# Forty modulation sums handed out anew over three stages of a two-block network

## What is computed

```python
def modulate(x, cond, norm_g, w_ada, b_ada):
    shift, scale, gate = jnp.split(jax.nn.silu(cond) @ w_ada + b_ada, 3, axis=-1)
    return rms_norm_2(x, norm_g) * (1 + scale) + shift, gate

h, gate = modulate(x, c, ...)        # condition c
hc, gate_c = modulate(xc, c_ctx, ...)  # condition c_ctx; its gate is not used
```

```python
def sq_relu_mlp(h, w_up, w_down):
    return jnp.square(jax.nn.relu(h @ w_up)) @ w_down
```

## The kernel before

| place | tiles | sums |
|---|---|---|
| rec_out, behind step j = 0, 1, 2, 3 | 0 to 3 | 1 each |
| up0, units 0 and 1 | 4, 5 | 1 each |
| up0, units 3, 5, ... 13 (loop) | 6 to 11 | 2 each |
| up0, units 14 and 15 | 12, 13 | 1 each |
| down0, m = 0 and 1, two tiles each | 14 to 17 | 2 each, so 4 per m |
| down0, m = 2 to 7 | 18 to 23 | 2 each |

## Time and profile before

### The profile page before, as it was taken

How to read it: one execution, slowest core, us unless ns; L and a number is a source line. 1 busy time by engine, 2 the same in 40 slices (tenths; PEclk the granted TensorE clock), 3 DMA queues, 4 the chain that set the end, 5 groups by cost and what they waited for, 6 DMA issues and landing times.

```text
span 894.3 us, 17915 instructions
## 1 busy us (share of the span) xinstructions
PE 864.8 (97%) x6992; PEld 822.3 (92%) x6992; DVE 686.5 (77%) x1072; ACT 473.1 (53%) x697; POOL 132.9 (15%) x154
## 2 busy tenths in 40 slices
PE   6999999999999997899999999999999999999998
PEld 5998999999999985599999999989899899999998
DVE  4896678889977688667676667677758998997793
ACT  7783355555443356755655444363367556636641
POOL 6220000012311000000000122232203222013000
PEclk9999999999999997999999999999999999999999
DMA  9754576679998432045655656556545554645542
GB/s 346 249 193 157 185 253 225 232 261 289 283 262 208 155 131 95 1 142 185 209 194 188 212 191 189 186 182 210 167 143 165 166 175 133 187 145 188 182 149 95
DMA packets 46960, 167.86 MB, mean 188 GB/s; under 512 B 5776, under 2 KB 5920, under 8 KB 46640
## 3 DMA queue, kind: packets, MB, share of 16 engines
q1 hardware_dynamic: 40896, 146.82, 49.8%
q0 software_dynamic: 5856, 20.00, 7.9%
q10 hardware_dynamic: 144, 0.15, 0.1%
HBM read 165.50 MB, written 1.44 MB: 187 GB/s over the span
## 4 chain that ended last, share of the span: by engine, by line
PE 73%; DVE 14%; issue 5%; ACT 5%; DMA 2%; DVEq 0%; ACTq 0%; SPq 0%
PE bank L560 20%; PE bank L562 19%; PE bank L561 19%; PE bank L627 5%; DVE wlo L1327 4%; ACT whi L967 2%; DVE ada_prod L1487 2%; DVE ada_prod L1511 2%; PE bank L645 2%; PE bank L787 1%; DVE tq L1543 1%; PE bank L882 1%; PE bank L892 1%; DMA raw<-weights 1%; PE bank L841 1%
## 5 line engine op out<-in xcount | busy, mean ns | idle before, releaser
L1327 DVE TENSOR_TENSOR wlo<-raw,whi 128x1024 fp32r<-128x1024 f32 x260 | 319.9, 1264 | 95.9 <-ACT whi L967 94.8
L560 PE MATMUL bank<-xh,whi 128*128 128x256 f32 x1328 | 374.9, 282 | 4.6 <-DVE vv L1923 1.5
L562 PE MATMUL bank<-xh,wlo 128*128 128x256 f32 x1328 | 369.7, 278 | 0.0
L561 PE MATMUL bank<-xl,whi 128*128 128x256 f32 x1328 | 369.7, 278 | 0.0
L967 ACT ACTIVATE whi<-raw 128x1024 fp32r<-128x1024 f32 x260 | 265.6, 1052 | 141.9 <-PE bank L562 104.2
L560 PEld LDWEIGHTS bank<-xh,whi 128*128 128x128 f32 x1328 | 249.2, 188 | 15.3 <-issue 8.6
L561 PEld LDWEIGHTS bank<-xl,whi 128*128 128x128 f32 x1328 | 249.3, 188 | 0.2
L562 PEld LDWEIGHTS bank<-xh,wlo 128*128 128x128 f32 x1328 | 249.3, 188 | 0.0
L560 PE MATMUL bank<-hhi,whi 128*128 128x256 f32 x512 | 142.4, 278 | 1.2 <-DVE wlo L1327 1.2
L562 PE MATMUL bank<-hhi,wlo 128*128 128x256 f32 x512 | 142.1, 278 | 0.0
L561 PE MATMUL bank<-hlo,whi 128*128 128x256 f32 x512 | 141.9, 277 | 0.0
(11 more groups left out here) (283 smaller groups left out, 1038.2 us busy)
## 6 DMA issues: line engine op xcount, KB each, us to landing
raw<-weights SPq DMA_DIRECT2D x260, 512.0 KB, 4.5
ada_raw<-ada_w POOLq DMA_DIRECT2D x24, 512.0 KB, 4.6
plain<-plain_w SPq DMA_DIRECT2D x16, 512.0 KB, 7.0
relB<-rel_scratch POOLq DMA_DIRECT2D x8, 256.0 KB, 7.3
bl<-rpb_in POOLq DMA_DIRECT2D x32, 64.0 KB, 3.7
x<-x_in SPq DMA_DIRECT2D x4, 256.0 KB, 6.2
cond<-cond_in POOLq DMA_DIRECT2D x1, 1024.0 KB, 7.8
cx<-ctx_in POOLq DMA_DIRECT2D x1, 1024.0 KB, 8.2
```

The source lines that it names most:

```text
L560: mmul(dst, hi, rh, start=start, stop=False)
L561: mmul(dst, hi, rlo, start=False, stop=False)
L562: return mmul(dst, lo, rh, start=False, stop=stop)
L1327: V_.tensor_tensor(wlo[:, sl], raw[:, sl], whi[:, sl].bitcast(F32), ALU.subtract)\
```

## The change

The total of 40 sums stays. The eight gate rows, which need one condition, all stand beside `rec_out`: tiles 0 and 1 ahead of step 0, then two behind each of the steps 0, 1 and 2, none behind step 3. `up0` gets one row of two conditions in each odd unit (tiles 8 to 15), and each tile of `down0` one row of two conditions (tiles 16 to 23). POOL loads tiles 2 to 9 in a row, then `cx`, then tiles 10 to 17.

```diff
-ADA_ORDER = [16, 17, 18, 19, 20, 21, 0, 1, 2, 3, 4, 5, 22, 23, 6, 7, 8, 9, 10, 11, 12, 13, 14, 15]
+ADA_ORDER = [16, 17, 18, 19, 20, 21, 22, 23, 0, 1, 2, 3, 4, 5, 6, 7, 8, 9, 10, 11, 12, 13, 14, 15]
-ADA_DOWN = [[14, 15], [16, 17], [18], [19], [20], [21], [22], [23]]
+ADA_UP, ADA_DOWN = 8, 16
...
-            for i in range(2, 6):
+            for i in range(2, ADA_UP + 2):
                 load_ada(i)
 
             pool.wait_ge(S_["chunk_used"], 2 * U0["up0"])
             pool.dma_start(cx[:], ctx_in).then_inc(S_["ctx_loaded"], 16)
-            quads(pool, U0["up0"], U0["up0"] + NUNITS["up0"], lambda q, r: load_ada_beside(q, r, U0["up0"]))
+            for i in range(ADA_UP + 2, ADA_DOWN + 2):
+                load_ada(i)
...
                 if isinstance(q, int):
-                    ada_tile({0: 4, 1: 5, 14: 12, 15: 13}[q * 4 + r - u0])
+                    if n % 2:
+                        ada_tile(ADA_UP + n // 2)
...
+            ada_tile(0)
+            ada_tile(1)
             for j in range(4):
                 add_to_x("rec_out", j, x[:, 2 * j:2 * j + 2])
                 x_lo(2 * j, "g_mlp0", 8 + 2 * j + 1)
                 x_lo(2 * j + 1, "g_mlp0", 8 + 2 * j + 2)
                 add_pair(0, j)
-                ada_tile(j)
+                if j < 3:
+                    ada_tile(2 * j + 2)
+                    ada_tile(2 * j + 3)
...
                     if name == "0":
-                        ada_tile(ADA_DOWN[m][0])
+                        ada_tile(ADA_DOWN + m)
...
-                    if name == "0" and len(ADA_DOWN[m]) > 1:
-                        ada_tile(ADA_DOWN[m][1])
```

More of the change, by code:

```diff
@@ L385, in load_ada @@
                 pool.dma_start(ada_raw[:, i % 2], ada_w[i]).then_inc(s_adaw[i % 2], 16)
[L387 to L396, removed]
             def zero_acc(k):
@@ L461, in load_rel_bias @@
                     .then_inc(S_["rel_bias_loaded"], 16)
[L463 to L466, removed]
             def add_ctx_squares(m):
@@ L479, in ahead_of_tile @@
                 add_ctx_squares(m)
-                if ADA_DOWN[m][0] + 2 < ADA_M:
-                    load_ada(ADA_DOWN[m][0] + 2)
+                if ADA_DOWN + m + 2 < ADA_M:
+                    load_ada(ADA_DOWN + m + 2)
             pool.dma_start(wiw[:], wi_in).then_inc(S_["wi_loaded"], 16)
             pool.wait_ge(S_["rel_stored"], 16)
-            squares_by_tile(3, 0, ahead_of_tile, behind_tile)
+            squares_by_tile(3, 0, ahead_of_tile, load_rel_bias)
             pool.dma_start(caus[:], c_caus).then_inc(S_["caus_loaded"], 16)
@@ L1501, in ada_beside @@
             def ada_beside(q, r, u0):
+                n = q * 4 + r - u0
                 if isinstance(q, int):
-                    ada_tile({0: 4, 1: 5, 14: 12, 15: 13}[q * 4 + r - u0])
+                    if n % 2:
+                        ada_tile(ADA_UP + n // 2)
                 elif r % 2:
-                    q0, a = u0 // 4 + 1, r // 2
-                    dve.wait_ge(s_adaw[a], q * 16 + 16 * (4 - q0))
-                    dve.wait_ge(S_["ada_used"], q * 2 + (6 + a - 2 * q0))
+                    q0, h = u0 // 4 + 1, r // 2
+                    i0 = ADA_UP + 1 + h
+                    dve.wait_ge(s_adaw[i0 % 2], q * 16 + 16 * (i0 // 2 + 1 - q0))
+                    dve.wait_ge(S_["ada_used"], q * 2 + (i0 - 2 * q0))
                     for c in range(2):
-                        V_.tensor_tensor_reduce(ada_prod[:], ada_raw[:, a], cond[:, c], 1.0, 0.0, ALU.mult, ALU.add,
+                        V_.tensor_tensor_reduce(ada_prod[:], ada_raw[:, i0 % 2], cond[:, c], 1.0, 0.0, ALU.mult, ALU.add,
                                                 ada_pair[:, c:c + 1]).then_inc(S_["ada_summed"], 1)
-                        dve.wait_ge(S_["ada_summed"], q * 4 + (2 * a + c + 1 - 4 * q0))
-                    V_.tensor_copy(ada[:, bass.ds(q * 2 + (a - 2 * q0), 1), :], ada_pair[:].unsqueeze(1))\
+                        dve.wait_ge(S_["ada_summed"], q * 4 + (2 * h + c + 1 - 4 * q0))
+                    V_.tensor_copy(ada[:, bass.ds(q * 2 + (1 + h - 2 * q0), 1), :], ada_pair[:].unsqueeze(1))\
                         .then_inc(S_["ada_used"], 1)
+            ada_tile(0)
+            ada_tile(1)
             for j in range(4):
```

## The result

The changed kernel took 896.81 us (median of 5, 896.31 to 898.25), the kernel of before 903.3 us (median of 5, 901.63 to 905.06): a ratio of 0.9932, 95% interval 0.9918 to 0.9945. (The ratios here are estimates of the record from all single times, not quotients of two medians.) Yet the two profiles don't differ by six microseconds anywhere.

What follows compares the result with a forecast made beforehand. VectorE was taken to set the time from 103 to 230 us, TensorE after. Gains of 1.0 us into up0 and 1.3 in down0, less 0.6 in up0's last unit, gave -1.7 us: 903.3 to 901.6 us, range 898.0 to 904.6.

Steps and rivals of the forecast that it cites:

- What bounds the kernel: From 103 to 230 us VectorE sets the time, though TensorE looks full; from 230.66 us TensorE does.
- rec_out, four sums at no cost: In rec_out, four more sums fit VectorE's waits for TensorE; the last ends before step 3 wants VectorE at 100.69 us.
- L: Time from issue to landing of an ada_raw load in rec_out: taken as 4.7 us, harmless up to 5.3 us.
- the formula itself: In rec_out, tile 7's sum ends no later than 80.1 + 3 x (load time + 0.3 + 1.24) us, unless its step holds it.
- Rival 1: Loads in rec_out come late, each us over 5.3 costing 3 in step 3; chance 0.15, 0.06 for slower than 906 us.
- Into up0, 1.0 us: Entering up0, an earlier raw load and one sum less ahead bring the loop's tq 1.05 us earlier; bounds 0 to 1.4.
- Last unit of up0, 0.6 us lost: Two sums in unit 15 delay the split of down0's fourth chunk; TensorE waits 0.6 us and restarts at 201.0.
- down0, 1.3 us gained: Fewer sums in down0's tiles 0 and 1 let TensorE run through; square sum at 237.7 us, or 236.5 at faster pace.
- From there on nothing changes: After the context's square sum TensorE sets the time at down0's end, so all later work moves with the gain.
- The gain does not hang on that, so it carries over: The 1.7 us gain holds whatever TensorE's pace in up1 and down1, so it comes off the 903.3 us median.
- rival 2: The change's restarts leave up1 and down1 at 113 ns, 5.9 us beside the 1.7: 895.7 us; chance 0.12.
- Same, 0.56: For the whole kernel, a chance of 0.56 that the measured time counts as the same, against faster 0.32 and slower 0.12.

Runs made afterwards that it cites:

- short-sums kernel: Kernel of before with each modulation sum made over 8 of its 1024 columns, loads as they were: 895.14 us, ratio 0.9972.
- thinned loads: Changed kernel with rec_out's ada_raw loads spread out, one at a time, and sums re-dealt in up0 and down0: 896.38 us, ratio 0.9992 to before.

## Why the prediction was right or wrong, point by point

- **What bounds the kernel**: right. VectorE sets the time from 103 to 230 us; its relief in the short-sums kernel moved the square sum by 6.2 us, in a trace with TensorE at the faster pace.
- **rec_out, four sums at no cost**: wrong, and the failed term is L. I took 4.7 us from rows in which one load of ada_raw travelled at a time, and wrote that the extra loads would meet "never a crowd"; the one issued at 88.09 stood beside a load of plain, two of raw and one of ada_raw. The chain shows 6.10 and 7.35, and the third load in the row took 3.79 at most (97.00 to 100.79). With these the formula itself is right: 84.7 + 6.10 + 7.35 + 3.79 = 101.94, the time of step 3's x. Rival 1 took place here, at the price of the early gain. The rule of the Trainium skill, "DMA: Bandwidth & Descriptors", section "Queues, rings and completion order", that an engine takes turns between queues, pointed the right way, and the 7.35, beside three loads of SP's queue, agrees with it. The 6.10 says less, since it was also issued 1.4 us behind another load of POOL's own queue.
- **Into up0, 1.0 us**: not gained, because of L. With thinned loads it was 0.90 us (121.60 to 120.70), and 1.17 (120.43) in the one trace of these sums with loads in time, so the working holds. One premise was wrong without harm: cx was issued at 102.84 us, took some 7.3, and so was not down before the raw load of 106.47; that load took some 6 us all the same.
- **Last unit of up0, 0.6 us lost**: right in place, smaller in size. TensorE restarted at 202.09 after a gap of 0.2 us beyond its usual step; it ran down0's first chunks at 118 ns, and I had reckoned with 113.
- **down0, 1.3 us gained**: the two waits are gone. With up0's missing 1.0 the square sum should have come at 238.7; it came at 238.94. (The 239.40 of rows 3 is where the chain enters the square sum; TensorE's timeline has its start at 239.24, so the forecast's gain was 0.16 us too large.)
- **"From there on nothing changes"**: wrong. The attention stage doesn't pass a gain on one to one, and TensorE's pace can change behind it. The profile after was 0.3 us ahead at 239, 0.4 behind at att_out (381.46 against 381.06), and ends 0.8 behind: the other 0.4 us are the 95 matmuls from 788 us on, which ran at 117.8 ns in the profile after and at 113 ns in the one before.
- **"The gain does not hang on that, so it carries over"**: this is the step by which the number fell out of the range: the base of 903.3 us, and that the pace would stay with it. I saw both paces, the price of 5.9 us and the 7.2 us between profile and median, and still set the base at 903.3 and gave rival 2 a chance of 0.12. The share of the faster pace was 77 of 109 executions of before over three sessions (22 of 33, 27 of 35, 19 of 29 and 9 of 12), and 22 of 29 of the changed kernel, the five of the result among them. (The five runs of before in the result are not among the 109.) A base of five executions all in the upper cluster was the rare thing, not the profile. Why those five were, stays open: if each execution fell by itself with that share, it would happen twice in a thousand times, so it was either rare luck or a condition of that session that no run here caught.
- **Rival 2, 895.7 us**: near the measured number, but by luck as far as the change goes. It had the change's restarts bring the faster pace and 1.7 us of the sums beside it; the kernel of before has that pace in 77 of 109 executions by itself, and the sums gave nothing that can be measured.
- **The effect of the change itself** is none that can be measured: 0.9996 and 0.9997 in two sessions, both intervals within 0.35%. "Same, 0.56" named that; the result as measured was faster.

## What to carry to other kernels

Before a difference of under one per cent is explained by an edit, look at the single times: two clusters with nothing between them, in one and the same program, mean that something differs between its executions, and then the edit has to be judged within a cluster. When loads are doubled up in a window, take their time from rows in which as many travel together, list what else is under way at each new issue, and put the margin (here 5.3 us) beside that. A gain ahead of a stage that runs at a falling and returning clock is not money in hand until it shows behind that stage. And one trace is one execution: here the four traces of the same sums had step 3's x at 100.57 to 102.75 us.

## What the runs showed of the hardware that was not expected

- TensorE streams the same pairs of weight load and 256-column matmul at 113.3 or at 117.8 ns, both at a granted clock of 1.00, and keeps one of them from a restart to the next: for 1508 matmuls in up1 and down1 in twelve traces, and in the thirteenth, with a restart between the two, on either side of it.
- The same program shows either pace in up1 (113 ns in 896.99 us, 118 ns in 903.98 us, both the changed kernel), but five kernels with one or two matmuls more at that restart never showed the faster, in 52 executions (five traces, the others by their times).
- In the attention stage a TensorE that came 1.6 and 3.0 us earlier needed up to 2.6 us longer (47.6 against 45.0 us), with a mean granted clock of 0.73 and 0.75 from 336 to 366 us where it had been 0.83; one that came 6.3 us earlier needed 1.0 us longer.
- The same load of ada_raw (512 KB, issued at about 88 us beside loads of plain and raw) took 6.6, 7.35, 7.8 and 8.1 us in four executions of the same sums; where none was issued into that crowd, in the kernel of before, they took 3.8 to 4.7.
